# First attention pair by eight half products from the rows themselves; operand sums all on VectorE; reciprocal by activations

## The reference, cut to what matters

```
u = rmsnorm(h, norm_mix[layer])
proj = u @ w_in[layer]
qa, ka, va, qd, kd, vd, z, beta_raw, a_raw, gate_raw = jnp.split(proj, split_at, axis=-1)
...
beta = jax.nn.sigmoid(beta_raw.astype(f32))
g = -jnp.exp(a_log[layer].astype(f32)) * jax.nn.softplus(a_raw.astype(f32) + dt_bias[layer].astype(f32))
```

## Time and profile before

| | |
|---|---|
| median of 3 runs | 2329.26 us (2327.79 to 2329.65) |
| the profiled execution | 2330.01 us, span 2328.3 us |
| TensorE busy | 2205.2 us, 95% |
| VectorE / ScalarE / POOL busy | 1079.8 / 937.3 / 694.2 us |
| TensorE in the chain that ended last | 87% |
| TensorE busy, first two slices of 58.2 us | five tenths each |
| TensorE busy, slices 3 to 29 | nine tenths |

### The profile page before, as it was taken

How to read it: one execution, slowest core, us unless ns; L and a number is a source line. 1 busy time by engine, 2 the same in 40 slices (tenths; PEclk the granted TensorE clock), 3 DMA queues, 4 the chain that set the end, 5 groups by cost and what they waited for, 6 DMA issues and landing times.

```text
span 2328.3 us, 30636 instructions
## 1 busy us (share of the span) xinstructions
PE 2205.2 (95%) x11016; PEld 1829.3 (79%) x11016; DVE 1079.8 (46%) x1470; ACT 937.3 (40%) x1597; POOL 694.2 (30%) x536
## 2 busy tenths in 40 slices
PE   5599999999999999999999999997899999999997
PEld 4488788787887888888888887885688888878886
DVE  6622331323237666656656543423755555550153
ACT  5344444444435545555654641122433333330012
POOL 6487565656522111111111124321000000043330
PEclk8799999999999999999999999998899999999999
DMA  5122212222132202211221343331122222261221
GB/s 111 29 60 68 74 55 65 87 69 74 55 94 80 64 18 72 63 36 45 63 61 29 127 150 114 93 87 45 55 82 81 81 81 81 81 223 48 89 56 73
DMA packets 249953, 175.64 MB, mean 75 GB/s; under 512 B 41272, under 2 KB 225784, under 8 KB 249872
## 3 DMA queue, kind: packets, MB, share of 16 engines
q1 hardware_dynamic: 219808, 136.46, 20.0%
q10 hardware_dynamic: 30064, 38.10, 5.2%
HBM read 143.36 MB, written 31.18 MB: 75 GB/s over the span
## 4 chain that ended last, share of the span: by engine, by line
PE 87%; DVE 5%; ACT 2%; issue 2%; DMA 1%; DVEq 1%; ACTq 1%; POOL 0%; SPq 0%; POOLq 0%
PE bank L213 20%; PE bank L2070 18%; PE bank L1013 16%; PE bank L2298 10%; PE bank L1218 5%; PE bank L1468 2%; PE bank L1451 2%; PE bank L701 1%; PE bank L1458 1%; DVE own_sum_t L488 1%; PE bank L712 1%; PE bank L1505 1%; PE bank L1500 1%; PE bank L1501 1%; PE bank L1487 1%
## 5 line engine op out<-in xcount | busy, mean ns | idle before, releaser
L213 PE MATMUL bank<-u_hi,w_hi 128*128 128x512 f32 x704 | 311.5, 442 | 6.1 <-ACT z_next L1685 4.8
L199 POOL CAST w_hi<-raw 128x1024 fp32r<-128x1024 f32 (+1 forms) x60 | 62.0, 1034 | 726.4 <-PE bank L213 511.6
L213 PE MATMUL bank<-u_hi,w_lo 128*128 128x512 f32 x704 | 277.0, 393 | 0.0
L213 PE MATMUL bank<-u_lo,w_hi 128*128 128x512 f32 x704 | 276.4, 393 | 0.0
L2258 POOL CAST dn_hi<-dn_raw 128x896 fp32r<-128x896 f32 (+1 forms) x24 | 26.0, 1085 | 590.6 <-DMA dn_raw<-in_w_down 482.3
L213 PEld LDWEIGHTS bank<-u_hi,w_lo 128*128 128x128 f32 x704 | 132.5, 188 | 29.3
L201 POOL TENSOR_TENSOR w_lo<-raw,w_hi 128x1024 fp32r<-128x1024 f32 (+1 forms) x60 | 149.0, 2483 | 8.6
L213 PEld LDWEIGHTS bank<-u_hi,w_hi 128*128 128x128 f32 x704 | 134.0, 190 | 22.2 <-ACT z_next L1685 5.3
L946 POOL TENSOR_TENSOR q_lo_s<-q_sum_s,q_hi_s 128x512 fp32r<-128x512 f32 x96 | 125.5, 1312 | 79.9 <-ACT q_hi_s L985 74.2
L213 PEld LDWEIGHTS bank<-u_lo,w_hi 128*128 128x128 f32 x704 | 134.2, 191 | 14.9 <-issue 1.9
L2298 PE MATMUL bank<-v_hi,dn_lo 128*128 128x512 f32 x352 | 136.9, 389 | 0.0
(11 more groups left out here) (367 smaller groups left out, 5605.2 us busy)
## 6 DMA issues: line engine op xcount, KB each, us to landing
raw<-in_w_in SPq DMA_DIRECT2D x36, 512.0 KB, 3.9
raw_first<-in_w_in SPq DMA_DIRECT2D x24, 512.0 KB, 3.9
raw_second<-in_w_in SPq DMA_DIRECT2D x24, 512.0 KB, 4.6
row<-scr_rows ACTq DMA_DIRECT2D x24, 512.0 KB, 4.7
raw_gate<-in_w_gate SPq DMA_DIRECT2D x22, 512.0 KB, 4.0
raw_up<-in_w_up SPq DMA_DIRECT2D x22, 512.0 KB, 3.9
scr_v<-gate_out SPq DMA_DIRECT2D x44, 256.0 KB, 2.6
v_in<-scr_v SPq DMA_DIRECT2D x11, 1024.0 KB, 8.5
```

Source lines behind the costliest of these rows:

```text
L199: nc.gpsimd.tensor_copy(hi[:, 0:kt, :], raw[slot][:, 0:kt, :])
L213: last = nc.tensor.matmul(bank[dst][:, :], wpart[slot][wp][:, k, :], rhs[ap][:, k, half * HALF:(half + 1) * HALF], start=k == 0 and (wp, a ...
```

## The change

- The transposes of the setup are no longer interleaved with `beta_decay`; all 48 of its matmuls follow them.
- Pair 0 is no longer made by seven products with sums but as plain halves (`first_pair_pe`): four outputs of 24 matmuls, 96 matmuls, from parts a, c, b, d and the quarters of u. It has 32 steps, so the first group has 60 steps, and pair 1 begins at step 32. `first_pair_act` copies the four outputs and casts the parts of pair 1 between the copies.
- The sums t1, t3, t2, t4 (in this order) are all formed before VectorE does anything else; the casts of t2 and t4 are behind the first pair (j = 32 and 34), since t2 takes the place of a quarter that the first pair reads.
- The order of parts for every later pair is a, c, s1, s2, s4, s3, d. POOL forms s3 after low s4, and ScalarE casts both s4 and s3 at product d's step. SyncE's load of the next `raw_first` waits for the low part of s3.
- The decay steps move to j = 9, 16, 36, 50 (ScalarE), 10, 20, 42 (VectorE) and 52 to 55 (transposes). The reciprocal is now Ln of 1 + x and Exp of its negative on ScalarE.

```diff
-            part_high(act, 0, "a")
-            part_high(act, 0, "c")
+            for name in ("a", "c", "b", "d"):
+                part_high(act, 0, name)
             operand_cast(act, "t1")
...
+            operand_cast(act, "t3")
...
-            for o, first, second in (("t1", part(0, 1), part(0, 0)), ("t2", part(1, 1), by_chunk("t1")),
-                                     ("t3", part(1, 1), part(0, 1)), ("t4", part(1, 0), by_chunk("t2"))):
+            for o, first, second in (("t1", u_part(0, 1), u_part(0, 0)), ("t3", u_part(1, 1), u_part(0, 1)),
+                                     ("t2", u_part(1, 1), by_chunk("t1")),
+                                     ("t4", u_part(1, 0), by_chunk("t2"))):
...
-                if c >= KT // 2:
-
-                    if c == KT // 2:
-                        pe.wait_ge(ba_split, 1)
-                        pe.wait_ge(x_low, KT)
-                    for k in (2 * c - KT, 2 * c - KT + 1):
-                        beta_decay(0, k)
...
+            pe.wait_ge(ba_split, 1)
+            for half in range(2):
+                pe.wait_ge(x_low, KT * (half + 1))
+                for k in range(KT):
+                    beta_decay(half, k)
...
-            elif j == 14:
+            elif j == 16:
                 act.wait_ge(ba_vec, 1)
                 f(row_t[1][b8, :], row_t[0][b8, :], ACT.Exp, scale=-1.0)
                 f(row_t[1][a8, :], row_t[2][a8, :], ACT.Exp)
                 act.drain()
-                f(row_t[1][a8, :], row_t[1][a8, :], ACT.Ln, bias=1.0).then_inc(ba_act, 1)
+                f(row_t[1][a8, :], row_t[1][a8, :], ACT.Ln, bias=1.0)
+                f(row_t[1][b8, :], row_t[1][b8, :], ACT.Ln, bias=1.0)
+                act.drain()
+                f(rows[a8, :], row_t[1][b8, :], ACT.Exp, scale=-1.0).then_inc(ba_act, 1)
...
-            v.reciprocal(rows[a8, :], row_t[1][b8, :])
...
+            free("s2")
             g.tensor_tensor(s2, s1, ra, ALU.subtract).then_inc(qp["sum"], 1)
             pool.drain()
             low("s1", s1)
-            free("s3")
-            g.tensor_tensor(s3, ra, rb, ALU.subtract).then_inc(qp["sum"], 1)
-            pool.drain()
-            low("s3", s3)
             free("s4")
             g.tensor_tensor(s4, rc, s2, ALU.subtract).then_inc(qp["sum"], 1)
             pool.drain()
             low("s2", s2)
             low("s4", s4)
+            free("s3")
+            g.tensor_tensor(s3, ra, rb, ALU.subtract).then_inc(qp["sum"], 1)
+            pool.drain()
+            low("s3", s3)
             low("d", rd)
...
-        HIGH_STEP = {1: ("a",), 2: ("c",), 4: ("s1", "s2"), 5: ("s3",), 6: ("s4",)}
+        HIGH_STEP = {1: ("a",), 2: ("c",), 4: ("s1", "s2"), 6: ("s4", "s3")}
...
+            for wp, ap in PASSES:
+                last = nc.tensor.matmul(bank[D1 - half][:, :], (q_hi, q_lo)[wp][name][:, k % 4, :],
+                                        act_in[ap][:, k, half * HALF:(half + 1) * HALF],
+                                        start=k == 0 and (wp, ap) == PASSES[0], stop=k == 7 and (wp, ap) == PASSES[-1])
...
+            act.wait_ge(qp["done"], (2, 4, 6, 7)[o])
+            if o == 0:
+                act.wait_ge(qp["sums"], 4)
+                act.wait_ge(x_low, 2 * KT)
+            nc.scalar.activation(qk_t[0][o // 2][:, half * HALF:(half + 1) * HALF], bank[D1 - half][:, :], ACT.Copy,
+                                 scale=1.0 if o // 2 else float(P) ** -0.5).then_inc(qp["copied"], 1)
+            if o == 1:
+                part_high(act, 1, "a")
+                part_high(act, 1, "c")
+            elif o == 2:
+                part_high(act, 1, "s1")
+                part_high(act, 1, "s2")
+            elif o == 3:
+                part_high(act, 1, "s4")
+                part_high(act, 1, "s3")
```

More of the change, by code:

```diff
@@ L422, in setup_act @@
                     roots(1)
-            part_high(act, 0, "a")
-            part_high(act, 0, "c")
+            for name in ("a", "c", "b", "d"):
+                part_high(act, 0, name)
             operand_cast(act, "t1")
[L427 to L434, removed]
-        def operand_cast(act, o):
-            act.wait_ge(qp["sums"], 4 if o == "t4" else OPERAND[o])
-            if o == "t4":
-                act.wait_ge(qp["low"], 2)
+            operand_cast(act, "t3")
+        OPERAND = {"t1": 1, "t3": 2, "t2": 3, "t4": 4}
+        def operand_cast(act, o):
+            act.wait_ge(qp["sums"], OPERAND[o])
+            if o == "t2":
+                act.wait_ge(qp["done"], 7)
+            elif o == "t4":
+                act.wait_ge(qp["low"], 3)
             nc.scalar.activation(ops_hi[o], own_sum[o][:, :, :], ACT.Copy).then_inc(x_high, 1)
@@ L951, in attention_pool @@
             low("c", rc)
+            pool.wait_ge(qp["second"], 16 * (q + 1))
+            if q == 0:
+                low("b", rb)
+                low("d", rd)
+                pool.sem_inc(qp["sum"], 4)
+                return
             s1, s2, s3, s4 = [q_sum[f"s{i}"][:, :, :] for i in (1, 2, 3, 4)]
-            pool.wait_ge(qp["second"], 16 * (q + 1))
             free("s1")
@@ L1043, in dense_att_act @@
             take_act(act, q, m, dst, src, second)
-            if m == 0 and q:
+            if m == 0:
                 part_high(act, q, "d")
@@ L1057, in take_act @@
             act.wait_ge(qp["done"], 7 * q + m + 1)
-            if q == 0 and m == 0:
-                act.wait_ge(qp["sums"], 4)
             if p == 1 and m == 0:
@@ L1096, in nothing, with attention @@
             pass
-        def attention(eng, dense, side_, mix, extra):
+        def attention(eng, dense_first, dense, side_, mix, extra):
             for s in range(NSLOT):
@@ L1102, in attention @@
                     steps = att_steps((g + 2) % 3) if s or g else []
-                    for j in range(56):
-                        dense(eng, s, g, j)
-                        if s == 0 and g == 0:
+                    first = s == 0 and g == 0
+                    for j in range(60 if first else 56):
+                        if not first:
+                            dense(eng, s, g, j)
+                        elif j < 32:
+                            dense_first(eng, j)
+                        else:
+                            dense(eng, s, g, j - 4)
+                        if first:
                             extra(eng, j)
@@ L2477, in _ @@
             setup_pe(pe)
-            attention(pe, dense_att_pe, att_pe, nothing, decay_pe)
+            attention(pe, first_pair_pe, dense_att_pe, att_pe, nothing, decay_pe)
             delta_iteration(pe, 0, dense_delta_pe, [nothing] * 6, att_pe, nothing)
@@ L2497, in _ @@
             setup_act(act)
-            attention(act, dense_att_act, att_act, mix_act_engine, decay_act)
+            attention(act, first_pair_act, dense_att_act, att_act, mix_act_engine, decay_act)
             restore_act(act)
@@ L2515, in _ @@
             dve.wait_ge(consts, 3)
-            attention(dve, dense_att_vec, att_vec, mix_vec_engine, decay_vec)
+            dve.sem_inc(qp["added"], 3)
+            attention(dve, nothing, dense_att_vec, att_vec, mix_vec_engine, decay_vec)
             dve.wait_ge(qp["done"], 7 * NQ)
```

106 lines of the change are left out of this document (66 added, 40 removed).

## The result

The changed kernel takes 2341.52 us (median of 5 runs, 2338.96 to 2342.51) against 2329.26 before (5 runs): ratio 1.0052, 95% interval 1.0037 to 1.0067. It is slower by 12 us. The forecast was 2332.9 with a range to 2341, so the time lies just above the range, on the side of case 3. The profiled execution took 2339.89 us, its span is 2338.2 us; it is 9.9 longer than the profiled execution of before.

The account below looks back on a forecast made before the run. TensorE was taken as the bound, idle at the start behind VectorE's chain. A start gain of 19.4 us and a boundary cost of 23.0 summed to +3.6, giving 2332.9 us for the median, range 2319 to 2341.

Parts of the forecast that it names:

- case 3: Rival: start's chain of exponentials, casts and POOL's parts longer, pair 1's product s2 after 98; 2340 us, chance 0.2.
- (a) to (d): Start: VectorE's sums from 36.9 to 55.3, lows of t1 and t3 to 59.8, TensorE's first pair to 70.0.
- (e): Start: first decay part ends at 67.1, ScalarE's exponentials take 8.0 us, TensorE waits for output 2's copy at 75.7.
- Part 2: The 22 later pair boundaries: new part order makes ScalarE's work 3.26 us later; cost 23.0 us, bounds 12 to 30.
- Step (f) of part 1: Start: ScalarE and POOL hand each other pair 1's parts, then t2 is cast; product s2 begins at 90.8.
- part 1: The start: pair 1 ends at 107.9 instead of 127.3, a gain of 19.4 us, bounds 14 to 23.
- (a): Eight boundaries inside groups with 15-part attention steps: TensorE stalls for the copy of va_t, together 11.8 us.
- (b): Boundary inside the first group of three later slots: cast of d, before the mix loads, 2.1 us later; together 6.3.
- (c): Three boundaries before the second group, mix at work: copy of output a late by 0.9, 1.2, 1.9; together 4.0 us.
- (d): Other boundaries between groups: copy still in time, raw rows' later load leaves 0.3 us three times, 0.9 together.
- Case 4: Rival: no table load between Ln and Exp at the start, 2.6 us shorter; 2330.3 us, chance 0.1.
- Case 2: Rival: new part order nearly free at later boundaries, cost 8 in place of 23; 2318 us, chance 0.2.

Follow-up runs that it names:

- e1: The changed kernel with the old order of the parts and the new start kept: 2313.47 us, ratio 0.9935 to the kernel before.
- e2: The kernel before with nothing but the new order of the parts: 2360.56 us, ratio 1.0142 to the kernel before.
- e5: The changed kernel with POOL's sums of s4 and s3 ahead of the lows of s2 and s4: 2314.45 us, ratio 0.9947 to the kernel before.
- e3: The changed kernel with VectorE's second decay part replaced by two memsets, so decay rows are not computed: 2338.13 us in one run.
- e7: The changed kernel with ScalarE's mix loads issued at step 36 of a group instead of 33: 2348.01 us, ratio 1.0091 to the kernel before.
- e8_turns_behind: New start, old part order, t2's cast ahead of s3 and s4, ScalarE's logarithms and the rest of the start's decay chain moved later: 2305.79 us, ratio 0.9907.
- e4: The changed kernel with the reciprocal back on VectorE instead of Ln and Exp on ScalarE: 2338.05 us, ratio 1.0044 to the kernel before.

## Why the prediction failed, step by step

**What held.** The bound of the kernel, the split into two terms of opposite sign, and the place and mechanism of each. (a) to (d): the sums started at 36.80 (said 36.9) and ended at 55.2 (55.3), the last eight 0.685 each and 0.64 apart; the lows ended at 59.8. (e): the first decay part ended at 67.8 (67.1), the exponentials took 8.0 as said, both table loads stood, and output 2 was copied at 75.83 (75.7 at its end, so 0.7 late). Part 2: from the cast of s4 to the cast of s3 it is 3.25 to 3.29 us in the traces, 22 times, where 3.26 was worked out; e1 and e2 show that the order costs the 27.3 us, and e5 that this round trip is 23.3 of them. TensorE's waits for ScalarE's copies, 130 to 700 us, rose from 11.4 to 31.1 us, by the 20 that were said.

**Step (f) of part 1 was mis-sized.** It took POOL's operations at "1.3 to 1.45 each, VectorE beside it". With VectorE's second decay part beside them, low s2, low s4 and sum s3 took 2.4, 2.4 and 2.2. e3 gives 1.26, 1.26 and 1.29 without it. Of the 3.7 us by which product s2 was late, these three made 2.9 (from 80.0 to 87.1, where 79.2 to 83.4 was said). The other 0.8 were there before: the first decay part took 7.8 us in place of the 7.2 of step (e), and the copy of output 2 was 0.7 late by it. All of it reached TensorE, because the cast of t2 stood behind the cast of s3. The rows to see it were there: VectorE's sums took 1.7 us beside POOL and 0.68 without it, and a slowdown of one of the two should have been asked of the other as well. The price of 1.3 came from a place where VectorE ran its reciprocal (88.92 to 95.46), which the change takes away. POOL of the kernel before, 92 to 95 us:

```profile
93.21 1.26 POOL L965 TENSOR_TENSOR q_sum_s<-raw_first,q_sum_s 128x512 f32<-128x512 f32 x1
```

**Gain 15.6 instead of 19.4**, inside the bounds of 14 to 23.

**Part 2 was mis-sized by 4.3 us**, 27.3 instead of 23.0, inside its bounds of 12 to 30. (a): 13.6 us for the eight boundaries instead of 11.8 (the four in middle groups 5.4 for 4.4, the four in last groups 8.2 for 7.2; the prediction's own terms add up to 11.6). (b): 9.7 instead of 6.3, the largest miss. I took the shift of ScalarE's first copy for the whole delay there. That shift came out at 1.8, 1.6 and 1.6 us instead of 2.1, but the stretch from the first copy to the second grew as well, from 7.48, 6.99 and 7.02 us to 8.31, 8.25 and 8.73, since SyncE's row loads, issued later, now fall among the mix loads; e7 shows both durations of that issue. Together they make 2.6, 2.9 and 3.3 of the 3.0, 3.3 and 3.4 us that the three boundaries cost; the rest I leave open. (c): 3.1 instead of 4.0. (d): 0.9 as said.

**Part 2 had no term for the clock.** Before, TensorE's granted clock stays at the upper level from pair 1 to pair 23. In the changed kernel it falls to the lower one (0.50) twice, behind the waits of 2.45 and 2.92 us for the copies of va_t in pairs 13 and 19; behind the wait of 2.60 us in pair 7 it does not. Stretches of TensorE (bounds, us, busy (count), granted clock, DMA share, GB/s):

```profile
403.40:406.50 3.10, 3.08 (x7) 0.50 0.06 0
556.90:559.90 3.00, 3.00 (x8) 0.50 0.01 3
```

The products begin 0.43 us apart there in place of 0.23, about 1.4 us for each stretch by my estimate. Part of it is taken back at once: TensorE's next wait, for the copy of the gates in pair 13, is 0.25 us long in place of 1.49.

**The sum.** The two misses, 3.8 and 4.3, have the same sign and make 8.1 us; the forecast missed by 8.6. The terms were large and of opposite sign, and I combined their central values with a range narrower than their own bounds allow: -14 and +30 give 2345, and the range ended at 2341. Case 3 was the nearest (slower, through the casts and POOL's work meeting VectorE's, "every delay there goes to TensorE one for one"), but its point of decision, product s2 after 98, wasn't reached: it was 94.5. "Against: POOL is idle in that stretch" was true of the sums at 50 to 55 and false of the casts at 80 to 87.

**Case 4.** The loads at 69.99 and 73.46 stood, 1.28 us each. The Trainium skill, page "ScalarE: Activation LUTs", section "Table sets: the hidden batching unit", says that one set with both functions would need one load; the traces do not agree, and they decide: there is a load at each change from Exp to Ln and from Ln to Exp, in all kernels of this study that have the sequence.

**Case 2** is false by e2: the order alone costs 32 us.

## What to carry to other kernels

Where two engines hand each other pieces in turn, the order of the program on the engine that feeds the other decides: put what the other waits for (the sums) ahead of what nobody waits for yet (the lows). Two moved lines were worth 27 us here, 23 of them at the boundaries. When a saving of tens of microseconds at the start and a cost of about one microsecond at each of 22 boundaries come in one edit, measure them apart, since the kernel with only the first half was 15 us faster than before while both together were 12 slower. And before work is moved from one engine to another, look which of the two stands in front of what TensorE waits for next: the reciprocal left VectorE, which was not last, and went in front of a copy that was.

## What was not expected of the hardware

The rows show how POOL and VectorE disturb each other. POOL's 128x512 subtractions for pair 1 (low s2, low s4, sum s3) take 1.26 to 1.29 us alone, in e3, and 2.2 to 2.4 beside VectorE's decay part. In e8_turns_behind an addition of the same size took 3.27 us (at 91.10) beside VectorE's scan (at 90.08, 3.20 us). VectorE's own 8x1024 instructions stretch too: the scaling by -1 of line 609 takes 1.61 us in the changed kernel and 0.68 in e4, where POOL is idle at that time. VectorE's reciprocal did not disturb POOL. POOL in e4_reciprocal, while VectorE's reciprocal runs from 74.61 for 6.54 us:

```profile
75.64 1.28 POOL L969 TENSOR_TENSOR q_sum_s<-raw_first,q_sum_s 128x512 f32<-128x512 f32 x1
77.08 2.54 POOL L948 TENSOR_TENSOR q_lo_s<-q_sum_s,q_hi_s 128x512 fp32r<-128x512 f32 x2 [0.16 <-issue]
79.57 1.29 POOL L974 TENSOR_TENSOR q_sum_s<-raw_first,raw_second 128x512 f32<-128x512 f32 x1
```

The Trainium skill, page "SBUF — State Buffer", section "Who interferes with whom", says that a VectorE instruction with two inputs from SBUF, or in one of its two-port modes, contends with GpSimd for shared ports, and that one with a single input outside these modes doesn't. The traces agree: the reciprocal, with one input, left POOL at 1.27 to 1.29, and the scan and the subtraction of line 612, with two, didn't. The scaling of line 609 has one input and was stretched as well; whether it ran in a two-port mode no row tells.

The second is the issue of DMAs on ScalarE. The five lines of the mix loads take 7.0, 6.8 and 7.2 us at the three boundaries of the changed kernel, with SyncE's two row loads issued 0.6 and 1.9 us after their start, and 5.9, 5.4 and 5.4 before, with one of the two ahead of them. They take 4.4 to 4.5 us in e7, where both row loads are ahead of them, and the same behind pair 23 of both kernels, where there are none. The lines that are stretched are the ones behind the row loads' issue. So what one queue issues and what another one's issue takes go together here; what in it slows is not shown.
